# Gate and up as one product of 512 columns in an expert layer on one core

## The reference

```python
logits = (x @ w_router + b_router); top_val, top_idx = top_k(logits, 4)
gate = softmax(top_val)
def expert_block(args):
    xe, e = args
    gt = jnp.minimum(xe @ w_gate[e] + b_gate[e], SWIGLU_LIMIT)
    up = jnp.clip(xe @ w_up[e] + b_up[e], -SWIGLU_LIMIT, SWIGLU_LIMIT)
    h = gt * jax.nn.sigmoid(SWIGLU_ALPHA * gt) * (up + 1.0)
    return h @ w_down[e] + b_down[e]
# every token gets the sum of its four experts' rows, weighted by gate; then a layer norm
```

## Time and profile before

| | us |
|---|---|
| median of 3 runs | 1459.44 (1458.39 to 1459.88) |
| profiled execution | 1456.15 |
| its span | 1454.4 |
| PE busy | 1358.7 |
| DVE busy | 583.3 |
| ACT busy | 269.9 |

### The profile page before, as it was taken

How to read it: one execution, slowest core, us unless ns; L and a number is a source line. 1 busy time by engine, 2 the same in 40 slices (tenths; PEclk the granted TensorE clock), 3 DMA queues, 4 the chain that set the end, 5 groups by cost and what they waited for, 6 DMA issues and landing times.

```text
span 1454.4 us, 41463 instructions
## 1 busy us (share of the span) xinstructions
PE 1358.7 (93%) x17038; PEld 766.0 (53%) x17039; DVE 583.3 (40%) x1111; ACT 269.9 (19%) x563; POOL 112.8 (8%) x327
## 2 busy tenths in 40 slices
PE   7999999999969999999999999999898998869994
PEld 5777674576544455555555555555454544335552
DVE  1069994451174333333333333333332333223335
ACT  0111113241111121112111211121111111111122
POOL 3400000000001100010000100100000000000100
PEclk9999999999978999999999999999999999999997
DMA  8333233516778970697997997999999999999991
GB/s 246 122 137 136 95 138 114 181 59 264 283 332 355 428 315 0 285 427 328 423 426 323 426 424 322 428 427 425 426 425 428 427 427 424 428 426 426 425 424 58
DMA packets 63026, 458.63 MB, mean 315 GB/s; under 512 B 4370, under 2 KB 7042, under 8 KB 30203
## 3 DMA queue, kind: packets, MB, share of 16 engines
q1 hardware_dynamic: 62714, 457.98, 76.8%
q10 hardware_dynamic: 289, 0.33, 0.1%
HBM read 454.09 MB, written 4.73 MB: 315 GB/s over the span
## 4 chain that ended last, share of the span: by engine, by line
PE 75%; DMA 18%; DVE 3%; SPq 2%; issue 1%; ACT 1%; ACTq 0%; DVEq 0%
PE PS L1299 21%; DMA SB<-in_w_down_dram 17%; PE PS L1025 14%; PE PS L1367 12%; PE PS L1322 6%; PE PS L1280 5%; PE PS L1005 3%; PE PS L1177 2%; PE PS L1118 2%; PE PS L1073 2%; PE PS L1197 2%; SPq L240 2%; PE PS L1305 1%; PE PS L1309 1%; DMA SB<-in_w_in_dram 1%
## 5 line engine op out<-in xcount | busy, mean ns | idle before, releaser
L1299 PE MATMUL PS<-SB 128*32 128x256 f32 x7424 | 432.6, 385 | 38.9 <-DMA SB<-in_w_up_dram 22.3
L1299 PEld LDWEIGHTS PS<-SB 128*32 128x32 f32 x7424 | 236.7, 111 | 217.4 <-issue 55.6
L922 DVE SCALAR_TENSOR_TENSOR SB<-PS,SB 128x1024 f32<-128x1024 f32 x177 | 194.9, 1101 | 83.1 <-PE PS L1322 83.1
L1367 PE MATMUL PS<-SB 128*32 128x256 f32 x3712 | 214.2, 381 | 7.3 <-DMA SB<-in_w_down_dram 7.3
L1025 PE MATMUL PS<-SB 128*128 128x320 f32 x768 | 209.2, 435 | 4.2 <-DMA SB<-in_w_in_dram 4.2
L1025 PEld LDWEIGHTS PS<-SB 128*128 128x128 f32 x768 | 146.8, 191 | 65.4 <-issue 5.5
L932 DVE TENSOR_SCALAR PS<-PS 128x256 f32<-128x256 f32 x58 | 25.1, 432 | 380.7 <-PE PS L1309 380.7
L1367 PEld LDWEIGHTS PS<-SB 128*32 128x32 f32 x3712 | 113.7, 110 | 89.7 <-DMA SB<-in_w_down_dram 11.9
L1322 PE MATMUL PS<-SB 32*128 32x256 f32 (+1 forms) x1416 | 124.8, 422 | 4.0 <-DVE SB L922 3.4
L669 DVE SCALAR_TENSOR_TENSOR SB<-SB 128x350 f32<-128x350 f32 x240 | 118.6, 572 | 0.0
L1280 PE MATMUL PS<-SB 128*32 128x256 f32 (+1 forms) x1416 | 98.1, 391 | 0.0
(11 more groups left out here) (214 smaller groups left out, 893.8 us busy)
## 6 DMA issues: line engine op xcount, KB each, us to landing
SB<-in_w_gate_dram SPq DMA_DIRECT2D x64, 2048.0 KB, 27.3
SB<-in_w_up_dram SPq DMA_DIRECT2D x64, 2048.0 KB, 32.6
SB<-in_w_down_dram SPq DMA_DIRECT2D x64, 2048.0 KB, 34.6
SB<-in_w_in_dram SPq DMA_DIRECT2D x14, 2048.0 KB, 8.0
SB<-in_w_pw_dram SPq DMA_DIRECT2D x2, 2048.0 KB, 9.9
SB<-in_w_att_o_dram SPq DMA_DIRECT2D x2, 2048.0 KB, 7.9
SB<-in_w_out_dram SPq DMA_DIRECT2D x2, 2048.0 KB, 8.2
SB<-rev_bias SPq DMA_DIRECT2D x2, 1024.0 KB, 8.4
```

Of the source, the lines that this page charges most:

```text
L922: dve.scalar_tensor_tensor(y, ps, gcol[:, tt:tt + 1], y, ALU.mult, ALU.add).then_inc(sem("yadd"), 1)
L1299: ins = pe.matmul(PS[32 * q:32 * q + 32, bank, 0:256], xg[:, c % 2, c // 2, :], buf[:, c, 256 * q:256 * q + 256], start=(c == 0), stop=False)
L1367: ins = pe.matmul(PS[32 * n:32 * n + 32, 2, 256:512], hT[:, ck % 2, ck // 2, :], WD[par][:, ck, 256 * n:256 * n + 256], start=(ck == 0), s ...
```

## The change

The gate and up matrices of one expert now lie so that one access pattern reaches both (buffers 1 and 2, or 0 and 3). Per chunk and quadrant one product of 512 columns, 256 of gate and 256 of up, goes into bank 0. `combine(i, 0)` stands behind chunk 0 and `combine(i, 1)` behind chunk 3. The bias sums have 512 columns each. VectorE does all of SwiGLU after both, writes the limited gate to SBUF, and takes over the copy of hT from ScalarE; the sigmoid goes from SBUF to SBUF. The rank broadcast is one product of 320 columns and stands ahead of the transposes of h. Before the loop SyncE loads up, gate and down for the first expert and gate, down and up for the second. In the loop it asks for the halves in pairs: gate and up first halves once both are read (`gu_half`), then the second ones (`gu_read`), then down.

```diff
-        WG, WU, WD = (wbuf[2], wbuf[0]), (wbuf[1], wbuf[5]), (wbuf[4], wbuf[3])
+        WG, WU, WD = (wbuf[1], wbuf[0]), (wbuf[2], wbuf[3]), (wbuf[4], wbuf[5])
+        every = SB[:, 0:6 * WB].rearrange("p (m c n) -> p m c n", m=6, c=KC)
+        WGU = every[:, 1:3], every[:, 0:4:3]
...
+        sg = view(M0 + 512, 256)
...
-                    load_halves(sp, WG[par], weights(wg_v, e), f"wg{par}", ["gate_half", "gate_done"], used)
-                    load_halves(sp, WU[par], weights(wu_v, e), f"wu{par}", ["up_half", "up_done"], used)
-                    load_halves(sp, WD[par], weights(wd_v, e), f"wd{par}", ["down_half", "down_done"], used)
+                    for h, read in enumerate(("gu_half", "gu_read")):
+                        sp.wait_ge(sem(read), used)
+                        load_half(sp, h, WG[par], weights(wg_v, e), f"wg{par}")
+                        load_half(sp, h, WU[par], weights(wu_v, e), f"wu{par}")
+                    for h, read in enumerate(("down_half", "down_done")):
+                        sp.wait_ge(sem(read), used)
+                        load_half(sp, h, WD[par], weights(wd_v, e), f"wd{par}")
...
             def turned():
-                act.copy(xg, PS[:, 3, 256:512].rearrange("p (j q s) -> p j q s", j=2, q=Q)).then_inc(sem("xg_ready"), 1)
+                act.copy(xg, PS[:, 0, 0:256].rearrange("p (j q s) -> p j q s", j=2, q=Q)).then_inc(sem("xg_ready"), 1)
...
                 act.wait_ge(sem("gmin"), i + 1)
-                act.wait_ge(sem("trx_mm"), i + 1)
-                act.activation(tin, PS[:, 0, 0:256], ACT.Sigmoid, scale=SW_ALPHA).then_inc(sem("sig"), 1)
+                act.activation(sg, tin, ACT.Sigmoid, scale=SW_ALPHA).then_inc(sem("sig"), 1)
                 act.wait_ge(sem("trh_mm"), i + 1)
-                act.copy(hT, PS[:, 3, 0:256].rearrange("p (j q s) -> p j q s", j=2, q=Q)).then_inc(sem("hT_ready"), 1)
...
-                    dve.wait_ge(sem("gate_done"), i + 1)
-                    dve.tensor_scalar(PS[:, 0, 0:256], PS[:, 0, 0:256], LIMIT, None, ALU.min).then_inc(sem("gmin"), 1)
+                    add_tile(i, 0)
+                    add_tile(i, 1)
+
+                    dve.wait_ge(sem("gu_done"), i + 1)
+                    dve.tensor_scalar(tin, PS[:, 0, 0:256], LIMIT, None, ALU.min).then_inc(sem("gmin"), 1)
+                    dve.tensor_scalar(PS[:, 0, 256:512], PS[:, 0, 256:512], LIMIT, -LIMIT, ALU.min, ALU.max).then_inc(sem("upc"), 1)
                     dve.wait_ge(sem("sig"), i + 1)
-                    dve.tensor_tensor(tin, tin, PS[:, 0, 0:256], ALU.mult).then_inc(sem("gsig"), 1)
...
+                    dve.tensor_tensor(tin, tin, sg, ALU.mult).then_inc(sem("gsig"), 1)
...
+                    dve.scalar_tensor_tensor(tin, PS[:, 0, 256:512], 1.0, tin, ALU.add, ALU.mult).then_inc(sem("h_ready"), 1)
+
+                    dve.wait_ge(sem("trh_mm"), i + 1)
+                    dve.tensor_copy(hT, PS[:, 3, 0:256].rearrange("p (j q s) -> p j q s", j=2, q=Q)).then_inc(sem("hT_ready"), 1)
                     add_tile(i, 2)
...
-                    dve.tensor_scalar(scat[:, 0:256], PS[:, 0, 256:512], slotcol[:, bass.ds(b, 1)], None, ALU.is_equal)
-                    dve.tensor_scalar(scat[:, 256:T], PS[:, 1, 256:256 + NS_], slotcol[:, bass.ds(b, 1)], None, ALU.is_equal)\
-                       .then_inc(sem("scat_ready"), 1)
+                    dve.tensor_scalar(scat, PS[:, 1, 0:T], slotcol[:, bass.ds(b, 1)], None, ALU.is_equal).then_inc(sem("scat_ready"), 1)
...
+            def gate_up(par, c):
+
+                for q in range(Q):
+                    ins = pe.matmul(PS[32 * q:32 * q + 32, 0, :].rearrange("p (w n) -> p w n", w=2), xg[:, c % 2, c // 2, :],
+                                    WGU[par][:, :, c, 256 * q:256 * q + 256], start=(c == 0), stop=False)
+                return ins
...
                         pe.wait_ge(sem("xg_ready"), i + 1)
-                        pe.wait_ge(sem("gsig"), i + 1)
-                        pe.wait_ge(sem("scat_ready"), i + 1)
-                        gate_or_up(0, WG[par], f"wg{par}", q * 16 + 16, 0, "gate_half", "gate_done", i * 2 + 2)
-                        pe.wait_ge(sem("y_sb"), i + 1)
-                        combine(i, 0)
-                        pe.wait_ge(sem("h_ready"), i + 1)
-                        gate_or_up(1, WU[par], f"wu{par}", q * 16 + 16, 1, "up_half", "up_done")
-                        combine(i, 1)
+                        for c in range(KC):
+                            if c % 4 == 0:
+                                pe.wait_ge(sem(f"wg{par}_{c // 4}"), q * 16 + 16)
+                                pe.wait_ge(sem(f"wu{par}_{c // 4}"), q * 16 + 16)
+                            if c == KC - 1:
+                                pe.wait_ge(sem("hot_ready"), i * 2 + 2)
+                            ins = gate_up(par, c)
+                            if c == 0:
+                                pe.wait_ge(sem("y_sb"), i + 1)
+                                pe.wait_ge(sem("scat_ready"), i + 1)
+                                combine(i, 0)
+                            if c == 3:
+                                ins.then_inc(sem("gu_half"), 1)
+                                combine(i, 1)
+                            if c == KC - 1:
+                                ins.then_inc(sem("gu_read"), 1)
+                        gate_up_bias()
...
                         gather(sel)
 
-                        pe.wait_ge(sem("hT_ready"), i + 1)
+                        who = hot16[:, 0:1].broadcast_to([E, P])
+                        pe.matmul(PS[:, 1, 0:T], who, rankT, start=True, stop=True).then_inc(sem("bc_mm"), 1)
+
                         pe.wait_ge(sem("h_ready"), i + 2)
```

More of the change, by code:

```diff
@@ L232, in apart, with load_half @@
             eng.wait_ge(sem("tables_done"), 1)
-        def load_halves(eng, buf, src, name, used=None, count=None):
+        def load_half(eng, h, buf, src, name):
             step = src.shape[1] // 2
[L237 to L240, removed]
+            eng.dma_start(buf[:, 4 * h:4 * h + 4, :], src[:, step * h:step * h + step, :]).then_inc(sem(f"{name}_{h}"), 16)
         def weights(v, e):
@@ L313, in _ @@
             sp.wait_ge(sem("p_mm"), PAIRS)
-            load_halves(sp, WG[0], wg_v[0], "wg0")
+            for h in range(2):
+                load_half(sp, h, WU[0], wu_v[0], "wu0")
             sp.wait_ge(sem("o_mm"), PAIRS)
@@ L342, in _ @@
                     e = sp.value_load(order[0:1, bass.ds(q * 2 + par, 1)], min_val=0, max_val=E - 1)
[L343 to L345 removed]
+                    for h, read in enumerate(("gu_half", "gu_read")):
[5 more added lines that the diff above has]
+                        load_half(sp, h, WD[par], weights(wd_v, e), f"wd{par}")
             used = sp.value_load(tbl[0:1, E - 1:E], min_val=1, max_val=200)
[L348 removed]
+            sp.wait_ge(sem("gu_read"), used)
             sp.dma_start(WG[0][:, 0, :], ln2_g.broadcast_to([P, D])).then_inc(sem("ln2_in"), 16)
@@ L1287, in turn_x @@
                 for j in range(2):
-                    ins = tr(PS[:, 3, 256 + P * j:256 + P * j + P], tin[:, P * j:P * j + P])
+                    ins = tr(PS[:, 0, P * j:P * j + P], tin[:, P * j:P * j + P])
                 ins.then_inc(sem("trx_mm"), 1)
-            def gate_or_up(bank, buf, loaded, count, which, half, done, hot_count=None):
-                for c in range(KC):
-                    if c % 4 == 0:
-                        pe.wait_ge(sem(f"{loaded}_{c // 4}"), count)
-                    if c == 4 and hot_count is not None:
-                        pe.wait_ge(sem("hot_ready"), hot_count)
-                    for q in range(Q):
-                        ins = pe.matmul(PS[32 * q:32 * q + 32, bank, 0:256], xg[:, c % 2, c // 2, :],
-                                        buf[:, c, 256 * q:256 * q + 256], start=(c == 0), stop=False)
-                    if c == KC // 2 - 1:
-                        ins.then_inc(sem(half), 1)
+            def gate_up(par, c):
[3 more added lines that the diff above has]
+                return ins
@@ L1303, in gate_or_up, with gate_up_bias @@
+            def gate_up_bias():
                 for q in range(Q):
                     r = slice(64 * (q // 2), 64 * (q // 2) + 64)
-                    pe.matmul(PS[32 * q:32 * q + 32, bank, 0:256], hot[r, 0:1].broadcast_to([64, SLOTS]), bias_hm[r, which, q % 2, :],
-                              start=False, stop=False)
+                    pe.matmul(PS[32 * q:32 * q + 32, 0, :].rearrange("p (w n) -> p w n", w=2), hot[r, 0:1].broadcast_to([64, SLOTS]),
+                              bias_hm[r, :, q % 2, :], start=False, stop=False)
@@ L1307, in gate_or_up @@
                 for q in range(Q):
                     r = slice(32 * q, 32 * q + 32)
-                    ins = pe.matmul(PS[r, bank, 0:256], hot[r, 0:1].broadcast_to([32, SLOTS]), bias_lo[r, which, :],
-                                    start=False, stop=True)
-                ins.then_inc(sem(done), 1)
```

(6 more changed lines are left out.)

22 lines of the change are left out of this document (11 added, 11 removed).

## The result

The changed kernel takes 1474.42 us (median of 4 runs, 1472.46 to 1476.39), the kernel before 1459.48. The ratio is 1.0104, with a 95% interval of 1.0086 to 1.0121: it is slower by some 15 us. 1474 was forecast. "Changed" is this kernel from here on, "before" the other one.

A forecast was written before the change was run, and what follows sets the result against it. Bound by PE to 882.39 us (tied with DMA in the 4-block groups), DMA to 1302.0, then PE. Stage terms gave +14.2 us at block 16.06, +15.2 at 16.1; +14.5 taken, 1474 on the runs' median, range 1462 to 1484.

The forecast's parts named there:

- The block: One expert block on PE, product to product: 16.06 us forecast against 16.00 before, bounds 15.5 and 16.5.
- the sum: Block parts added up to 16.06 us; over the whole kernel, stage differences added up to +14.2 us at that block.
- The chain on the path: SwiGLU after the second bias sum takes 2.37 us, PE has 2.02 us meanwhile, so the transposes of h wait 0.35 us.
- The release: First gate half handed back later in a block: issue at 4.56 us instead of 2.12, 2.44 later wherever the DMA is idle.
- The block's share: Longer blocks where PE decides: at 16.1, +0.5 us for five blocks and +0.8 for the last eight.
- The low clock: Granted clock falling to the low level in new waits of 2 to 4 us at the 4-block experts; part of rival 4.
- rival 4: Block 16.4 us or more, from ysb, the chain or the clock in new waits: +23 us or more, 1483; chance 0.08.
- the up half decides, by 0.34 us: After the fourth landing: 11.93 us of block left against 11.59 for the last down half, with block 16.1.
- The four stages: To 510.27 us loading; to 882.39 PE, tied with DMA in groups; to 1302.0 DMA; then PE: +14.2 us at 16.06.
- Rivals 1 and 2: First: block 15.55 to 15.85, chain covered, +3 to +9 us, chance 0.15; second: block near 15.4, within 2.9 us, 0.08.
- Rival 3: Gate and up product: matmuls have a fixed price, half as many pay half; faster, block below 15.25 us; chance 0.09.
- Rival 5: Only the later release, block unchanged at 16.0 us: +12.8, 1472; inside the forecast, joint chance 0.60.

The follow-up runs named there:

- after_extra_op: The changed kernel with one more VectorE operation (h times 1.0) in the SwiGLU chain: 1481.16 us, ratio 1.0151 to before.
- before_extra_op: The kernel before with the same additional VectorE operation ahead of its last SwiGLU product: 1459.02 us, ratio 1.0001.
- before_late: The kernel before, with SyncE asking for gate's first half only when the whole gate product and bias are done: 1469.25 us, ratio 1.0073.
- after_small_loads: The changed kernel with only a small piece of each half loaded in the loop, 30 of 32 experts' matrices left out: 1413.05 us.
- merges_behind_half: The changed kernel with the first merge moved behind chunk 3 and the signal gu_half, the second behind chunk 5: 1472.11 us, ratio 1.0087 to before.

## Why the prediction was right

- **The block.** 16.06 from the sum, 16.05 measured. Its parts: second bias sum at 8.81, measured 8.87; from it to the transposes 2.37, measured 2.29, because the step between the last two operations is 0.46, not the 0.54 taken from another pair; from there to the next block 4.88, measured 4.89. That 512 columns save nothing over two of 256 held: the half product from 539.52 to 543.09 takes 3.57 us with its change of tile, just what a whole one of 256 columns took in the earlier trace rows.
- **The chain on the path.** Shown by after_extra_op, and by before_extra_op for the other side.
- **The release.** 4.56 us forecast, 4.61 measured, 2.5 later than before. before_late carries it alone, and by its 5.0 us per us this is 12.3 of the 16.7 us.
- **The block's share.** 0.05 us in 58 blocks is 2.4 us without the supply (after_small_loads). In the full kernel it counts some 20 times (after_extra_op), 1 us.
- **The low clock** behind the new waits cost 2.3 and 1.2 us in the profiled execution. With release and block that makes 16.8 us, against 16.7. The prediction had it only in rival 4, with 0.08.
- **Wrong: "the up half decides, by 0.34 us".** The prediction left 16.1 - 4.17 = 11.93 us of the block behind the fourth landing. But 4.17 us is when the first halves have been read, and the second merge still stands ahead of the wait for the second halves, as the order of TensorE's rows above shows. The second half starts at 4.97 us (534.55 to 539.52), and 11.08 are left (539.52 to 550.60). The down half takes 11.61 (654.94 to 666.55) and decides: TensorE waits 0.33 us for it at 664.80, and the chain names it at 664.80, and again at 1319.83. The same is seen where the order was changed: in merges_behind_half, with one merge ahead of that wait, up decides. The sum has 0.34 in five places (0.30 at 16.06). Without them, and with the rest as it stands, it gives some +12.8 instead of +14.2.
- **The four stages.** They gave +14.2, the profile has +16.7: 2.3 more in the first, 0.7 more in the groups, 0.5 less behind them. The 1.5 us too much for the up half hide a part of the 3.5 left out for the clock, which is luck. So in part is the 1474: the medians differ by 14.9, the profiled executions by 20.2, of which 3.2 lie ahead of the experts. How much the other executions of changed lost to the low clock is not shown, since only one has a trace.
- **Rivals 1 and 2** needed a shorter block, at most 15.85 and near 15.4. It is 16.05, and the chain is not covered. **Rival 3**, a fixed price per matmul: half as many products brought nothing in a stream (3.46 us for the half product of 512 columns, 539.52 to 543.09 less the change of tile, against 3.45 for a whole one of 256). **Rival 5**, only the release, was the largest part of it.

Not tried: keeping TensorE busy through the new waits, which would show whether the fall of the clock can be avoided.

## What to carry to other kernels

Where transfers wait for buffers, the time until a buffer's first part is given back is paid once for each stretch in which the DMA runs dry; count these stretches before you put other work ahead of the signal, or signal first and merge afterwards. Where the array already streamed without gaps, the product twice as wide saved nothing here; what it cost were the results that used to be worked on under the second product. When you ask which of two landings decides, count what stands ahead of each wait in the engine's own queue, not only what has been read. And a balance of transfer and compute is read from the end: see which of them was ready first, and order the work so that neither has a rest left.

## What the runs showed of the hardware

- A change of tile shape costs TensorE some 0.11 us, an estimate from two steps: from one 16-bit bias sum to the next it takes 0.22 us with 256 columns (529.84, 530.05) and 0.33 with 512 (543.09, 543.42). So 256 more columns take 0.11 us, and 0.11 of either step are not columns.
- Waits for a landing can bring the granted clock down to 1.2 GHz, but a wait's length did not tell whether it does. In changed the half products behind waits of 3.79 and 2.34 us were slow (6.41 and 5.27 us instead of 3.57), that behind one of 3.08 (1044.31) was not. In merges_behind_half a wait of 2.39 us was followed by the high clock. In before, with waits of at most 1.7 us from 460 to 880, the clock stayed at 2.4 GHz.
- Two loads of 1 MB in place of one of 2 MB made the stretch of full DMA 0.07 us longer for each pair: 0.95 us for 14 pairs in before's form, 2.0 for 28 in the changed one.
- A VectorE operation with one SBUF source of 128 x 256 fp32 took 0.29 us (L949 of after_extra_op), with two sources 0.42 to 0.43.
